# A row of modulation summed inside the up-projection loop, a convolution tap on ScalarE, and two output products on a shared bank

## The reference, cut to what matters

```python
mod = silu(c) @ w_ada + b_ada                # 6 rows of 1024
sh1, sc1, ga1, sh2, sc2, ga2 = split(mod, 6)
h  = rms_norm(x, g_mix) * (1 + sc1) + sh1    # and the same for ctx
x  = x + ga1 * (merge(s5(h, hc), sgu(h), gates(h)) @ w_out)
h2 = rms_norm(x, g_ffn) * (1 + sc2) + sh2
up = depthwise_conv3x3(h2 @ w_up)            # 1024 -> 2 * 2816, on a 4 x 64 grid
gate, val = split(up, 2)
x  = x + ga2 * ((silu(gate) * val) @ w_down) # 2816 -> 1024
out = rms_norm(x, g_final)
```

## Time and profile before

| what | value |
|---|---|
| runs, median (lowest to highest) | 472.12 us (471.29 to 472.27) |
| profiled execution, device time | 472.59 us |
| its span, first to last instruction | 470.8 us |
| TensorE busy | 97% |
| VectorE busy | 86% |
| ScalarE busy | 22% |
| GpSimd busy | 10% |
| mean granted TensorE clock | 0.985 |

### The profile page before, as it was taken

One profiled execution on the slowest core, in us unless ns is written; L12 is line 12 of the kernel. 1 busy time (PEld: TensorE's weight loads), 2 busy tenths in 40 slices (PEclk: granted clock), 3 DMA queues, 4 the chain that ended last, 5 costly groups with the idle time before them and its releaser, 6 DMA issues.

```text
span 470.8 us, 7801 instructions
## 1 busy us (share of the span) xinstructions
PE 455.9 (97%) x2671; PEld 351.1 (75%) x2671; DVE 403.5 (86%) x836; ACT 105.9 (22%) x198; POOL 48.1 (10%) x77
## 2 busy tenths in 40 slices
PE   8899999989999899999989999999999999999994
PEld 5677857888888788885468888887888887444454
DVE  4598999999999867789755999998999999899644
ACT  5423355135104005201161111011011111200002
POOL 2001100003013232100000111010011011000000
PEclk9899999999999969999999999999999999999999
DMA  8994499633999999993986543452443443000002
GB/s 296 419 419 144 130 340 170 223 144 81 111 274 402 411 397 399 402 412 135 427 318 253 179 166 116 166 180 94 173 178 112 155 178 137 41 0 1 0 1 89
DMA packets 22091, 97.41 MB, mean 207 GB/s; under 512 B 6504, under 2 KB 7152, under 8 KB 13360
## 3 DMA queue, kind: packets, MB, share of 16 engines
q1 hardware_dynamic: 15024, 74.70, 44.0%
q0 software_dynamic: 5632, 20.71, 13.8%
q10 hardware_dynamic: 1408, 1.63, 1.0%
HBM read 94.44 MB, written 2.59 MB: 206 GB/s over the span
## 4 chain that ended last, share of the span: by engine, by line
PE 77%; DVE 16%; DMA 3%; issue 2%; ACT 1%; SPq 0%; DVEq 0%; ACTq 0%
PE bank L764 31%; PE bank L775 14%; PE bank L565 11%; DVE s_region L1043 8%; PE bank L672 6%; PE bank L716 4%; PE bank L480 4%; DMA gates<-early_w 3%; PE bank L653 2%; PE bank L693 1%; DVE s_region L1162 1%; PE bank L445 1%; DVE s_region L1300 1%; DVE gates L1043 1%; DVE s_region L1331 1%
## 5 line engine op out<-in xcount | busy, mean ns | idle before, releaser
L764 PE MATMUL bank<-h_all,s_region 128*128 128x256 f32 x704 | 152.6, 379 | 0.9 <-ACT ctx_region L992 0.7
L764 PEld LDWEIGHTS bank<-h_all,s_region 128*128 128x128 f32 x704 | 133.1, 190 | 20.2 <-ACT ctx_region L992 1.1
L1571 DVE SCALAR_TENSOR_TENSOR ctx_region<-ctx_region,pk_sb 128x189 f32<-128x189 f32 (+2 forms) x352 | 127.5, 439 | 0.2 <-DVE ctx_region L1571 0.2
L565 PE MATMUL bank<-h_all,ring_region 128*128 128x256 f32 x256 | 58.2, 389 | 0.5 <-DVE s_region L1331 0.5
L565 PEld LDWEIGHTS bank<-h_all,ring_region 128*128 128x128 f32 x256 | 49.8, 196 | 8.3 <-DVE s_region L1331 0.7
L775 PE MATMUL bank<-s_region,ring_region 128*128 128x512 f32 (+1 forms) x132 | 47.6, 521 | 0.0
L775 PEld LDWEIGHTS bank<-s_region,ring_region 128*128 128x128 f32 x132 | 25.1, 190 | 22.6 <-issue 21.5
L992 ACT ACTIVATE ctx_region<-bank 128x512 f32<-128x512 f32 x22 | 13.2, 599 | 126.1 <-PE bank L764 69.7
L1043 DVE TENSOR_TENSOR s_region<-s_region,power 128x2048 f32<-128x2048 f32 (+1 forms) x16 | 38.1, 2421 | 0.2
L397 POOL TENSOR_TENSOR ring_region<-gates,ctx_region 128x256 f32 x22 | 17.3, 785 | 181.2 <-ACT gates L997 181.2
L1561 DVE TENSOR_SCALAR ctx_region<-ctx_region,pk_sb 128x256 f32<-128x256 f32 x44 | 21.1, 522 | 13.2 <-ACT ctx_region L992 12.1
(11 more groups left out here) (241 smaller groups left out, 518.0 us busy)
## 6 DMA issues: line engine op xcount, KB each, us to landing
s_region<-up_w SPq DMA_DIRECT2D x33, 1024.0 KB, 4.8
ring_region<-ring_w SPq DMA_DIRECT2D x22, 1024.0 KB, 9.0
s_region<-mod_w POOLq DMA_DIRECT2D x22, 512.0 KB, 13.9
s_region<-early_w SPq DMA_DIRECT2D x4, 1024.0 KB, 21.8
s_region<-out_w SPq DMA_DIRECT2D x4, 1024.0 KB, 12.7
h_all<-mod_w POOLq DMA_DIRECT2D x6, 512.0 KB, 16.6
gates<-early_w SPq DMA_DIRECT2D x2, 1024.0 KB, 10.8
s_region<-k_scratch POOLq DMA_DIRECT2D x8, 256.0 KB, 12.0
```

Source lines behind the costliest of these rows:

```text
L565: mx = pe.matmul(bank[5 - j % 2][:, mm * TOK:(mm + 1) * TOK], ring[:, u % RING, (mm * KD + k) * P:(mm * KD + k + 1) * P], h_x[:, k, :], st ...
L764: mx = pe.matmul(bank[s % 3][:, half * TOK:(half + 1) * TOK], up_ring[:, s, (half * KD + k) * P:(half * KD + k + 1) * P], h2[:, k, :], sta ...
L1571: dve.scalar_tensor_tensor(out=o, in0=a, scalar=cw[:, tile[half], (dy + 1) * 3 + dx + 1], in1=o, op0=ALU.mult, op1=ALU.add).then_inc(s_con ...
```

## The change

1. All eight tiles of `ga2` become dot products on VectorE inside the up loop: one after every second tile of the first 16 (`LATE_UNITS`). `MT` falls to 24, so four sums leave the stages before; the two ring units, their products, copies and picks go. The weights of the eight (`late_load`, 512 KB each, two buffers) and the broadcast `c` are loaded from ScalarE's queue, and ScalarE takes its silu behind tile 1.
2. The summed `ga2` is stored to a scratch row in DRAM as 1,024 single floats at ScalarE's step 19, and loaded back broadcast at step 21. The diagonals, the products L781 and the two copies go.
3. The centre tap of the gating half moves from VectorE to ScalarE (scale and bias of an activation), behind the copy of the same tile; VectorE has 17 instructions per tile.
4. `s_upsb` starts at 2, and the first tile of round 1 waits for the copy of tile 9 in place of 10.
5. Output products: order 1, 5, 6, 2, 7, 3, 4, 8; 6 and 7 add onto bank 1, copied after 1 and after 6, and 3 onto bank 4. The third block of `w_out` is summed with its sign turned, so that 4 and 8 are added. The tiles are scaled by `ga1` piece by piece, which leaves two in place of three steps behind 4 and 8. The squares of half 1's second part are taken ahead of those of half 0's second part, and `x_hat` of half 0 after product 3.
6. The last store is issued by ScalarE.

```diff
-        OUT_BANK = {1: 1, 2: 1, 3: 4, 5: 4, 6: 6, 7: 5, 4: 7, 8: 0}
+        OUT_BANK = {1: 1, 6: 1, 7: 1, 5: 4, 3: 4, 2: 6, 4: 7, 8: 0}
...
-            for n in range(ROW_UNITS):
-                later_rows(n)
-            for n in range(ROW_UNITS):
-                later_pick(n)
...
-                    pe.wait_ge(s_upsb, r * USLOTS + max(1, s - 1))
+                    pe.wait_ge(s_upsb, r * USLOTS + (1, 2, 2)[s] if s < 3 else r * USLOTS + s)
...
-            for f in range(2):
-                mx = pe.matmul(bank[2 + f][:, :], ones[:, :], ga2_diag[:, 4 * f:4 * f + 4, :].rearrange("p k n -> p (k n)"), start=True, stop=True)
...
             row_squares(0, x1_tok[:, 0, 0, :], 512)
-            row_squares(1, x1_tok[:, 0, 1, :], 512)
-            row_root(0, 1)
+            row_squares(1, x1_tok[:, 1, 1, :], 512)
+            row_squares(2, x1_tok[:, 0, 1, :], 512)
+            row_root(0, 2)
...
+                    act.wait_ge(s_upsb, j + 3)
+                    act.activation(conv[:, j % 2, 0:TOK], up_sb[:, j % 2, 0:TOK], ACT.Identity, scale=cw[:, j, 4:5],
+                                   bias=par("conv_b")[:, j:j + 1]).then_inc(s_tap, 1)
...
+                elif j % 2 == 0 and 4 <= j < 4 + 2 * (KD - 2):
+                    t = j // 2
+                    act.wait_ge(s_mt_used, MT + t - 1)
+                    late_load(t)
+                elif j == LATE_UNITS + 3:
+                    act.wait_ge(s_ga2, 1)
+                    act.dma_start(ga2_dram[:].rearrange("a (k p) -> p (a k)", p=P), mod2[:, MT:4 * KD], allow_slow_non_contiguous=True).then_inc(s_ga1_out, 16)
+                elif j == LATE_UNITS + 5:
+                    act.wait_ge(s_ga1_out, 32)
+                    act.dma_start(ga2_bc, ga2_dram[:].partition_broadcast(P).rearrange("p a (k n) -> p (a k) n", k=KD)).then_inc(s_early[3], 16)
...
-            tt(out_s[1], out_s[0], m11, ALU.subtract)
-            settle()
-            dve.tensor_tensor(out_s[2], m12, out_s[1], ALU.subtract).then_inc(s_so, 1)
-            dve.tensor_tensor(m21, m11, m21, ALU.subtract).then_inc(s_so, 1)
-            modulation_sums(26, 28)
+            dve.tensor_tensor(out_s[1], out_s[0], m11, ALU.subtract).then_inc(s_so, 1)
...
+            scaled_by_ga1(1, 1, copy16)
+            tt(x1_tok[:, 0, 1, :], x1_tok[:, 0, 1, :], scaled_out[:, 1, :], ALU.add)
...
+            with dve.Fori(0, LATE_UNITS // 4) as i:
+                for b in range(4):
+                    convolved(i * 4 + b, b % 2)
+                    if b % 2 == 1:
+                        dve.wait_ge(s_cbc, 2)
+                        dve.wait_ge(s_early[b // 2], i * 16 + 32)
+                        dve.scalar_tensor_tensor(out=late_tile[b // 2], in0=late_tile[b // 2], scalar=1.0, in1=c_late, op0=ALU.mult, op1=ALU.mult,
+                                                 accum_out=mod_late[:, bass.ds(i * 2 + b // 2, 1)]).then_inc(s_mt_used, 1)
```

More of the change, by code:

```diff
@@ L52 @@
 U_PROJ = U_GLU + 1
[L53 to L56, removed]
+UNITS = U_PROJ + 4
+MT = 3 * KD
 MTS = 9
@@ L142, in build @@
         x1_tok = s5_region[:, USLOTS * UNIT:USLOTS * UNIT + 2 * D].rearrange("p (h f n) -> p h f n", h=2, f=2)
+        c_late = gate_region[:, 512:512 + D]
+        late_tile = [gate_region[:, 512 + (b + 1) * D:512 + (b + 2) * D] for b in range(2)]
         t1_homes = [gate_region[:, 512:4096].rearrange("p (s n) -> p s n", s=7), u_x[:, :].rearrange("p (s n) -> p s n", s=2),
@@ L715, in out_product @@
                         pe.wait_ge(s_mg, 2 * i + 1)
-                    mx = pe.matmul(bank[OUT_BANK[n]][:, cols], lhs(i), rhs(i)[:, cols], start=(i == 0 and n not in (2, 3)), stop=(i == KD // 2 - 1),
+                    mx = pe.matmul(bank[OUT_BANK[n]][:, cols], lhs(i), rhs(i)[:, cols], start=(i == 0 and n not in (3, 6, 7)), stop=(i == KD // 2 - 1),
                                    skip_group_check=True)
@@ L944, in _ @@
                                bias=par("b_glu")[:, m:m + 1]).then_inc(s_glu, 1)
-            def last_rows(n):
-                act.wait_ge(s_unit, U_ROWS + n + 1)
-                act.activation(rows1[:, n % 2, :], bank[LATER_BANK[n]][:, 2 * P:4 * P], ACT.Copy).then_inc(s_rows, 1)
             preload_sqrt()
-            for i, n in enumerate((1, 5)):
+            for i, n in enumerate((1, 5, 6)):
                 act.wait_ge(s_po, i + 1)
@@ L997, in _ @@
                     act.activation(silu_sb[:, (j - 1) % 2, :], conv[:, (j - 1) % 2, 0:TOK], ACT.Silu).then_inc(s_silu, 1)
+                if j == 1:
+                    act.wait_ge(s_early[2], 32)
+                    act.activation(c_late, c_late, ACT.Silu).then_inc(s_cbc, 1)
+                elif j % 2 == 0 and 4 <= j < 4 + 2 * (KD - 2):
[8 more added lines that the diff above has]
+                    act.dma_start(ga2_bc, ga2_dram[:].partition_broadcast(P).rearrange("p a (k n) -> p (a k) n", k=KD)).then_inc(s_early[3], 16)
             preload_sqrt()
[L1001 to L1003 removed]
             act.wait_ge(s_act, KF + 2)
@@ new lines, in convolved @@
+            def convolved(j, b):
+                base = j * CONV_OPS
+                dve.wait_ge(s_upsb, j + 3)
+                dve.wait_ge(s_act, j + 1)
+                src = [up_sb[:, b, half * TOK:(half + 1) * TOK] for half in range(2)]
+                dst = [conv[:, b, half * TOK:(half + 1) * TOK] for half in range(2)]
+                tile = [bass.ds(j + KF * half, 1) for half in range(2)]
+                dve.tensor_scalar(dst[1], src[1], cw[:, tile[1], 4], par("conv_b")[:, tile[1]], ALU.mult, ALU.add).then_inc(s_conv, 1)
+                dve.wait_ge(s_tap, j + 1)
+                done = 1
+                for dy, dx in taps:
+                    r0, r1 = max(0, -dy), GRID_H - max(0, dy)
+                    c0, c1 = max(0, -dx), GRID_W - max(0, dx)
+                    for half in range(2):
+                        o = dst[half].rearrange("p (r c) -> p r c", c=GRID_W)[:, r0:r1, c0:c1]
+                        a = src[half].rearrange("p (r c) -> p r c", c=GRID_W)[:, r0 + dy:r1 + dy, c0 + dx:c1 + dx]
+                        if done > 1:
+                            dve.wait_ge(s_conv, base + (done - 1))
+                        dve.scalar_tensor_tensor(out=o, in0=a, scalar=cw[:, tile[half], (dy + 1) * 3 + dx + 1], in1=o, op0=ALU.mult,
+                                                 op1=ALU.add).then_inc(s_conv, 1)
+                        done += 1
```

155 lines of the change are left out of this document (60 added, 95 removed).

## The result

The changed kernel takes 468.02 us (median of six runs, 466.53 to 468.50) against 471.74 us of the kernel before in the same comparison (470.32 to 473.16): ratio 0.991, 95% interval 0.988 to 0.994. The forecast was 467.8 us. The profiled execution has a span of 466.2 us in place of 470.8.

What follows compares the result with a forecast made beforehand. TensorE was taken as the bound, busy 455.9 of 470.8 us, so gains come from its stream, waits and end. Terms 1.4 + 1.0 + 1.7 + 0.4 = 4.5 us gave 467.6, taken as 467.8 us; range 466.7 to 470.6.

Steps and rivals of the forecast that it cites:

- Output stage: Output products to up loop: new order starts the first up product at 242.3 in place of 243.67, -1.4 us.
- The removed thin products and picks lay inside TensorE's idle time: 0: Between output products and up loop: removing the thin products (238.45, 1.93 us) and picks gains nothing.
- Up loop, TensorE: Seam of the two rounds: waiting for tile 9's copy in place of tile 10's saves 1.0 us, or 0.
- Up loop, VectorE: Up loop: pairs of tiles take 14.2 to 14.4 us against TensorE's 13.82; covers absorb the lag, cost 0.
- rival C: VectorE leaves the cover: in-loop sums cost 2.8 us, TensorE waits about 9.8 us before product 3, 477.6 us; chance 0.06.
- ScalarE's tap, less than 0.60 us: Up loop: ScalarE's centre tap, half the width of its 0.60 us copy, takes less than that.
- Down products: Before the down products: TensorE's four ga2 records go, -1.7 us; product 3's activation sum keeps at least 1.6 us left.
- Queues: DMA queues: ScalarE's added loads and ga2's scattered store and load are hidden, cost 0.
- Rival D: Nothing changes: product 1 waits for a down weight or activation, -1.7 and -1.0 return as waits, 470.5 us; chance 0.04.
- End: Last store, issued by ScalarE beside SP, goes out one issue earlier: -0.4 us, between 0 and -0.5.
- Rival A, the clock: Gap before the up loop: TensorE's clock falls to 0.50, costing 1.0 to 1.7 us, 469.1 us; chance 0.27.

Runs made afterwards that it cites:

- order_alone: Kernel before with only the new output stage (banks, order, operand sums, scaling, squares), ring units of ga2 left in place: 472.40 us, ratio 1.000.
- wait_alone: Kernel before with only the new s_upsb threshold (starts at 2, first tile of round 1 waits for tile 9's copy): 470.32 us, ratio 0.996.
- tap_back: Changed kernel with both centre taps on VectorE, 18 instructions a tile: 469.69 us, ratio 0.995.
- tap_back_early: tap_back with ga2's scattered store at ScalarE's step 17 in place of 19 and its broadcast load at 19 in place of 21: 467.48 us, ratio 0.990.
- filler_again: The same kernel as filler_early, run once more beside a repeat of the changed kernel: 469.91 us, one run.
- filler_early: Changed kernel with three matmuls of constants in TensorE's idle time before the up loop, and ga2's store and load two tiles earlier: 468.09 us, ratio 0.990.
- filler_both: filler_early with two more matmuls of constants on bank 1 in TensorE's idle time at 14 us: 466.06 us, ratio 0.987.

## Why the prediction was right

**Output stage: -1.4 predicted.** Right in kind. x_hat of half 1 came 1.76 us earlier (steps on VectorE that need no wait overlap, 0.61 us apart where I charged up to 0.73), and the transposes gained another 0.2: 1.96 us with the clock held. With the clock fallen 0.77 are left. "The removed thin products and picks lay inside TensorE's idle time: 0" was true of the old order alone; order_alone shows that in the new one they cost 1.6 us and more.

**Up loop, TensorE: -1.0 predicted, 1.02 measured**, and shown by wait_alone.

**Up loop, VectorE: 0 predicted, 0 measured**, but the size of the backlog was wrong. I charged 14.2 to 14.4 us a pair; it is 13.84 (264.43 to 347.47 over six pairs). The step that failed is the sum over gaps: I added 0.11 and 0.32 us between tiles and register waits for the sum, where instructions that need no result of the one before start while it still runs: the next tile starts 1.14 us after the start of a sum that lasts 1.22. How much VectorE has to spare is less sure, as 13.84 is also TensorE's pace within 0.02 us; a VectorE that lags all the time, with one tap more a tile, needs 14.30 a pair (tap_back). Less two taps that is an estimated 13.7. VectorE ended 0.3 us later against the down products, for which 1.6 to 3.2 had been allowed. For rival C this was on the safe side, and tap_back_early shows how far: VectorE can take both taps. The step "ScalarE's tap, less than 0.60 us" was also low, it takes 0.60 at half the width.

**Down products: -1.7 predicted, 1.72 measured,** by the timeline (2.74 us less from the copy of tile 0 to the down products, 1.02 of them from the wait); no run takes the four records out alone.

**Queues: 0 predicted, 0 to 0.65 us measured.** Of the scattered store I asked when it lands. It lands in time. What I did not ask is what it does to the load behind it. Rival D names a wait of product 1 for a down weight and puts it aside, as the slots were filled long before; the last slots are not, and this is the only new wait of TensorE behind the start of the up loop.

**End: -0.4 predicted, +0.1 measured.** The issue was earlier, the landing later.

**Rival A, the clock,** had 0.27. It happened in the profiled execution and in three others of seven, and costs 1.2 us, inside the 1.0 to 1.7 predicted. Its chance should have been near one half.

**The sum.** From the first output product to the end it is 257.37 us before and 253.97 after: -3.4 with the clock fallen, and -4.6 where it held (filler_again and filler_early, 252.7 and 252.8). The forecast's terms add up to -4.5. The measured ones are -0.8 (-2.0 with the clock held), -1.0, -1.7 and +0.1: with the clock fallen, 1.1 us short. The remaining 1.2 us between the two spans is the first stage, whose clock fell at 16 us in the one profile and not in the other. The prediction has no term for it, and it made up what was short. In the medians the gain is 3.7 us (471.74 to 468.02) where 4.3 were forecast (472.12 to 467.8). So the forecast was met because a gain larger than foreseen in the output stage, a fall of the clock, a store worth nothing, a better first stage and a kernel before that ran 0.4 us faster this time nearly cancel. The mechanisms of the 1.0 and 1.7 us are shown; that the total agrees to 0.2 us is luck.

## What to carry to other kernels

Take work out of the stream of the engine that sets the pace and put it where another has room, then look whether what you took out had been in front of something: half of this change is worth nothing without the other half. Ask of a small scattered DMA what follows it in the queues, and place it where the next loads have slack. Where an idle stretch is left on TensorE ahead of its longest loop, a few matmuls on a free bank cost nothing (35.58 us with them and, where the clock held, without); filler_early and filler_both do the same work as the changed kernel in 1.2 us less from the output products on. Whether that shows in the median is another matter: filler_early has 468.09 us, as its first stage was late.

## What was not expected of the hardware

A 4 KB store in 1,024 pieces slowed a 1 MB load that was issued after its packets were gone: 12 packets in 2 us where the load ahead of it had moved 81; why is not shown, and in tap_back the slowest landing took 14.3 us for a median of 4.8. The granted clock fell in one and the same gap, around idle times of 0.52 and 1.22 us, in four executions of seven. ScalarE's Identity with scale and bias on 256 columns took 0.60 us, as long as its copy of 512 columns out of a bank, and its silu of 256 columns 0.40. Two 256 KB stores issued on two queues at once ended no earlier than one behind the other on a single queue.
